# Weight products as plain float32 matmuls and one weight stream over all stages, in a six-layer transformer on one core

## What is computed

```
def ec_moe(x, w_router, w_gate, w_up, w_down):
    aff = softmax(einsum('bnd,de->bne', x, w_router))
    gates, idx = top_k(swapaxes(aff, 1, 2), cap)
    xin = x[bidx, idx]
    h = silu(einsum('becd,edf->becf', xin, w_gate)) * einsum('becd,edf->becf', xin, w_up)
    out = einsum('becf,efd->becd', h, w_down) * gates[..., None]
    return zeros_like(x).at[bidx, idx].add(out)

def swiglu(h, w_gate, w_up, w_down):            # four times, 1024 -> 2816 -> 1024
    return (silu(h @ w_gate) * (h @ w_up)) @ w_down

proj = h @ w_in        # in every mixer, 1024 -> 1536 to 6656 outputs
y = mixed @ w_out      # in every mixer, 1024 to 2304 -> 1024
```

## Time and profile before

| | |
|---|---|
| median of 3 runs | 2966.36 us (2957.82 to 2967.57) |
| profiled execution, its span | 2972.5 us (the profile gives no other time for it) |
| TensorE busy | 2382.3 us, 80% of the span |
| VectorE, ScalarE busy | 1300.9 us, 980.6 us |
| mean granted TensorE clock | 0.884 of full |
| moved by DMA | 690 MB |

### The profile page before, as it was taken

How to read it: one execution, slowest core, us unless ns; L and a number is a source line. 1 busy time by engine, 2 the same in 40 slices (tenths; PEclk the granted TensorE clock), 3 DMA queues, 4 the chain that set the end, 5 groups by cost and what they waited for, 6 DMA issues and landing times. The chain is left out here.

```text
span 2972.5 us, 33569 instructions
## 1 busy us (share of the span) xinstructions
PE 2382.3 (80%) x13393; PEld 1740.5 (59%) x13393; DVE 1300.9 (44%) x2056; ACT 980.6 (33%) x1638; POOL 22.4 (1%) x18
## 2 busy tenths in 40 slices
PE   8887555657876656649888988899879999987998
PEld 7752111126642213118767777787768888875887
DVE  5630000035622000024664554675667567465674
ACT  4420000015510000013444433544555454433543
POOL 0010000000010000000000000000000000000000
PEclk9977778778978778777988999999999999987999
DMA  6469999974469999984423443454236545561453
GB/s 229 158 270 421 421 422 422 421 297 159 192 278 419 420 420 419 422 312 116 117 83 132 144 159 127 132 198 156 90 121 210 193 142 198 159 195 33 159 198 121
DMA packets 277072, 689.98 MB, mean 232 GB/s; under 512 B 22193, under 2 KB 181889, under 8 KB 227664
## 3 DMA queue, kind: packets, MB, share of 16 engines
q1 hardware_dynamic: 276944, 688.20, 61.6%
HBM read 687.09 MB, written 5.28 MB: 233 GB/s over the span
## 5 line engine op out<-in xcount | busy, mean ns | idle before, releaser
L339 DVE TENSOR_TENSOR weight_quarters<-weight_ring,weight_quarters 128x1024 fp32r<-128x1024 f32 (+4 forms) x512 | 605.6, 1190 | 578.9 <-ACT weight_quarters L328 566.0
L328 ACT CAST weight_quarters<-weight_ring 128x1024 fp32r<-128x1024 f32 (+4 forms) x512 | 520.6, 1022 | 699.2 <-PE accumulators L3283 242.1
L3281 PE MATMUL accumulators<-xT_halves,weight_quarters 128*128 128x512 f32 x1408 | 497.7, 398 | 9.3 <-DVEq L3337 9.3
L1671 PE MATMUL accumulators<-weight_ring,arena 128*32 128x512 f32 x2048 | 333.6, 812 | 202.5 <-DMA weight_ring<-in_moe_w_up 101.7
L3283 PE MATMUL accumulators<-xT_halves,weight_quarters 128*128 128x256 f32 x1408 | 396.9, 282 | 0.0
L966 PE MATMUL accumulators<-weight_quarters,arena_halves 128*128 128x512 f32 x1552 | 362.2, 394 | 8.8 <-PEq L220 8.8
L1671 PEld LDWEIGHTS accumulators<-weight_ring,arena 128*32 128x32 f32 x2048 | 87.8, 143 | 436.9 <-issue 436.2
L966 PEld LDWEIGHTS accumulators<-weight_quarters,arena_halves 128*128 128x128 f32 x1552 | 295.4, 191 | 72.0 <-issue 9.9
L3281 PEld LDWEIGHTS accumulators<-xT_halves,weight_quarters 128*128 128x128 f32 x1408 | 266.2, 189 | 72.6 <-issue 10.0
L2423 PE MATMUL accumulators<-xT_halves,weight_quarters 128*128 128x256 f32 x2040 | 276.9, 298 | 15.1 <-DVE weight_quarters L339 10.9
L2423 PEld LDWEIGHTS accumulators<-xT_halves,weight_quarters 128*128 128x128 f32 x2040 | 267.2, 205 | 22.0 <-issue 9.9
(11 more groups left out here) (429 smaller groups left out, 2096.7 us busy)
## 6 DMA issues: line engine op xcount, KB each, us to landing
weight_ring<-in_moe_w_gate SPq DMA_DIRECT2D x64, 2048.0 KB, 19.7
weight_ring<-in_moe_w_up SPq DMA_DIRECT2D x64, 2048.0 KB, 21.1
weight_ring<-in_moe_w_down SPq DMA_DIRECT2D x64, 2048.0 KB, 21.4
weight_ring<-in_ffn_w_gate SPq DMA_DIRECT2D x44, 1024.0 KB, 5.3
weight_ring<-in_ffn_w_up SPq DMA_DIRECT2D x44, 1024.0 KB, 7.8
weight_ring<-in_ffn_w_down SPq DMA_DIRECT2D x20, 2048.0 KB, 7.9
weight_ring<-in_l_w_in SPq DMA_DIRECT2D x13, 2048.0 KB, 7.6
weight_ring<-in_mlstm_w_in SPq DMA_DIRECT2D x6, 2048.0 KB, 7.8
```

Source lines behind the costliest of these rows:

```text
L328: act.copy(high, raw).then_inc(self.m.high_ready, 1)
L339: dve.tensor_tensor(low, raw, high, ALU.subtract).then_inc(self.m.low_ready, 1)
L1671: last = pe.matmul(acc[e * CAP:(e + 1) * CAP, half * BANK:(half + 1) * BANK], tokens, w4[e][:, c * D + half * BANK:c * D + (half + 1) * BANK],
L3281: pe.matmul(out.rearrange("p (x t) -> p x t", x=2), gs.quarter(k, 0)[:, c, :], m.xT_r[:, :, c, :], start=(c == 0), stop=False)
```

## The change

- **Products.** Every weight product, every score of the mLSTM and every gather becomes one plain float32 matmul from the operands as they are. All casts and differences go, with the quarters, `Order`, the cross terms of the feed-forward layers, and the parts of activations. Activations are written once into `xT`, by ScalarE for some chunks and VectorE for the others (`moved`).
- **Stream.** The ring has 13 slots of 8 KiB per partition (1 MiB). All units of all stages stand in one list, `m.units`, and unit i goes to slot i mod 13. `fill` lets SP issue loads up to 13 units ahead of a point, each waiting until the unit 13 before it is used. A unit is one or two pieces of a column block (4 or 8 channel chunks), two chunks of rows, half of a feed-forward pair, or 256 rows of one expert. The loops are unrolled.
- **Feed-forward.** Weights are stationary (128x128), the 256 tokens move; gate and up of a unit take one bank each; ScalarE's silu reads PSUM, VectorE multiplies straight into `hT`.
- **Experts.** Group 0 is gathered first, the other three together in two calls of 384 columns (`gather_rest`), behind steps 4 and 8 of group 0.
- **Order of loads.** The orders of outputs that casts made in the even layer are now made by the transfer (pieces of 64 columns). The first stage loads five units, not two, ahead of the constants. The bias tiles of the selected stage are issued by POOL, not SP; the memory rows of the second expert layer at its start.
- **Pool layer.** Its projection writes the transposed form directly, so the transposing stage and the stage of parts go.

The core of the diff:

```diff
-SLOTS = 6
-SLOT = 4096
+SLOTS = 13
+SLOT = 2048
+    def load_units(self, sp, end):
+        while self.issued < min(end, len(self.units)):
+            stream, u = self.units[self.issued]
+            if self.issued >= SLOTS:
+                sp.wait_ge(self.unit_used, self.issued - SLOTS + 1)
+            stream.load(sp, u)
+            self.issued += 1
...
-PASSES = ((0, 0), (0, 1), (1, 0))
...
 def out_matmuls(m, stream, pe, s, chunks, lhs, bank, hidden=None, before=None):
-        for n, (xp, wp) in enumerate(PASSES):
-            ins = pe.matmul(m.ps[:, bank + 2 * t + h, :], lhs(xp, i, t), stream.quarter(i % 4, wp)[:, h * BANK:(h + 1) * BANK],
-                            start=(first and n == 0), stop=(last and n == 2))
+        return pe.matmul(m.ps[:, bank + 2 * t + h, :], lhs(i, t), stream.slot(i // 2)[:, i % 2 * D + h * BANK:i % 2 * D + (h + 1) * BANK], start=first, stop=last)
...
     def quarter(self, pe, s, u, k):
-        stream.wait_low(pe, g, j, k)
-                for n, (xp, wp) in enumerate(PASSES):
-                    last = pe.matmul(self.block(u, i), stream.quarter(k, wp, self.width(u))[:, c, i * P:(i + 1) * P], m.xT_r[:, xp, 2 * k + c, :], ...
+        for c in (2 * k, 2 * k + 1):
+            stream.begin_chunk(pe, u, c)
+            def turned(i):
+                return pe.matmul(self.block(u, i), stream.chunk(u, c)[:, i * P:(i + 1) * P], m.xT[:, c, :], ...
...
 def ffn(m, gu_stream, down_stream, tail):
-                    for c in range(DC):
-                        pe.matmul(out.rearrange("p (x t) -> p x t", x=2), gs.quarter(k, 0)[:, c, :], m.xT_r[:, :, c, :], ...
-                        last = pe.matmul(out[:, T:2 * T], gs.quarter(k, 1)[:, c, :], m.xT_r[:, 0, c, :], ...
+                    for f in range(2):
+                        for c in range(DC):
+                            last = pe.matmul(out[:, f * T:(f + 1) * T], w[:, c, f * P:(f + 1) * P], m.xT[:, c, :], ...
+                act.activation(gate[:, u % 2, :], m.ps[:, u % 2 * 2, :], ACT.Silu).then_inc(s["silu_out"], 1)
...
 def moe(m, stream, layer, tail, under=None):
+            def gather_rest(r):
+                for c in range(HALF):
+                    last = gather(HALF * r + c, m.ps[:, 4 + c, 0:REST], slice(P, P + REST))
+                last.then_inc(s["gathered"], 1)
...
 def selected_attention(m, in_stream, out_stream, tiles, tail):
-            heads.load(sp, s, 0)
-            heads.load(sp, s, 1)
-            in_stream.load_rest(sp)
+            in_stream.fill(sp, in_stream.n)
+        @block.gpsimd
+        def _(pool):
+            pool.wait_ge(m.bias_stored, 32)
+            for i in range(len(units)):
+                heads.load(pool, s, i)
```

More of the change, by code:

```diff
@@ L228 @@
 class Stream:
[L232 to L254, removed]
-        m.queue.append(self)
@@ L257, in slot @@
[L257 to L338, removed]
-        dve.tensor_tensor(low, raw, high, ALU.subtract).then_inc(self.m.low_ready, 1)
-        if k == 3 or last:
-            dve.wait_ge(self.m.low_ready, q + 1)
-            dve.sem_inc(self.m.unit_used, 1)
@@ L457, with __init__, place, slot @@
-PASSES = ((0, 0), (0, 1), (1, 0))
+    def __init__(self, m, units):
+        self.m, self.parts, self.n, self.base = m, units, len(units), len(m.units)
+        self.full = []
+        for u, parts in enumerate(units):
+            m.units.append((self, u))
+            m.loads[self.place(u)] += 16 * len(parts)
+            self.full.append(m.loads[self.place(u)])
+        m.queue.append(self)
+    def place(self, u):
+        return (self.base + u) % SLOTS
+    def slot(self, u):
+        return self.m.ring[:, self.place(u), :]
@@ L977, in out_matmuls @@
             for h in range(2):
-                last = products(i, t, h, i == 0, False)
-        last.then_inc(m.quarter_used, 1)
-    stream.wait_low(pe, 0, 0, chunks - 1)
+                last = product(i, t, h, i == 0, False)
+        if i % 2 == 1:
+            last.then_inc(m.unit_used, 1)
+    stream.wait_loaded(pe, chunks // 2 - 1)
     if hidden:
@@ L1052, in _ @@
         def _(act):
-            for i in range(stream.ready_made, chunks):
-                stream.high_part(act, i // 8, i // 4 % 2, i % 4)
-            stream.high_ahead(act)
             tail.warm_root(act, s)
@@ L3358, in after @@
-            def after(k, g, j):
-                if k == 1:
-                    gate_sum(g, j)
-                if k == 3:
-                    hidden(g, j)
-            def unit(g, j):
-                for k in range(first(g, j), 4):
-                    gs.low_part(dve, g, j, k)
-                    if not (isinstance(g, int) and g == 0 and j == 0):
-                        after(k, *back(g, j))
-            gs.each(dve, unit, peel=True)
-            for i in range(FFC):
-                ds.low_part(dve, i // 8, i // 4 % 2, i % 4, last=(i == FFC - 1))
-                if i < 4:
-                    after(i, *end)
```

1202 lines of the change are left out of this document (395 added, 807 removed).

## The result

The changed kernel takes 3169.9 us (median of 4 runs, 3169.5 to 3171.6); the kernel before took 2967.0 us on the same chip. The ratio is 1.068, 95% interval 1.066 to 1.071: slower by 203 us, forecast +213. The profiled execution's span is 3169.8 us.

A forecast was written before the change was run, and what follows sets the result against it. TensorE was taken to bound most stages outside the expert layers, weight transfer those layers. Products +331, start +4, removed work and waits -122 give +213 us on 2966, about 3180 us, range 3115 to 3235 (0.70).

The forecast's parts named there:

- Price of the product: Weight products outside the experts: plain 0.4275 us per 256 columns, split gate/up 0.345; TensorE +331 us in sum.
- Feed-forward: Four feed-forward layers: gate and up +29 us, down +16 us each, +180 us in all; removing casts and subtractions worth nothing.
- Mixers' idle time: TensorE's waits in mLSTM, GLA, even, odd and selected: 68 of 115 us go, bounds 0 and 115.
- Half-clock stretches: GLA, even and selected, at lowered clock after waits: fewer waits give back about 15 us, bounds 0 and 40.
- After the expert layers: Tails: 11 us saved after the second expert layer, 4 after the first; SP's loads ahead cost 0, at most 5 a stage.
- Experts: Expert layers: a larger ring shortens the transfer that sets the end, 2.5 us saved each; merged gathers 0.
- Narrow rows: Two units of the even layer loaded in rows of 256 bytes: 0 taken, between 0 and 10 us.
- Pool, tails: Pool layer: three units +7 us, transposes and parts stage -7.5; seven RMS tails 1.7 us less each.
- Signs: Profile marks named beforehand: two records a product, 0.214 us a record, feed-forward layer 228 us, ScalarE and VectorE near 430 and 620.
- Rivals 1 and 2: Waits outside the expert layers vanish almost wholly, 3050 us (chance 0.12); the mixers' waits stay, 3255 us (chance 0.09).
- rival 3: Expert layers: weight stream slower with 1 MiB transfers, 386 GB/s instead of 420, 85 us more, 3265 us; chance 0.05.
- rival 4: Products outside the experts: a plain product costs half of what was counted, about 2400 us in all; chance 0.03.

The follow-up runs named there:

- experiment 2: Kernel before, three matmuls a product kept, casts and subtractions of weights narrowed to 8 columns from the first gated layer on: 2903.5 us, ratio 0.978.
- `before_light`: Kernel before with weight casts and subtractions narrowed to 8 columns of each row from the first gated layer on, matmuls and waits kept: 2903.5 us, ratio 0.978.

## Why the prediction was right, and where its terms were off

It forecast +213 us and +203 were measured, and the likeliest case was the one that happened: TensorE sets the stages outside the experts, the plain product costs what the old rows say, and some of the waits go. That the sum came out only 10 us off is in part luck: the loads ahead of two stage ends cost 29 us more than forecast, and three other terms gave back 42 us more.

- **Price of the product.** 0.4275 us was read from a few old products; 0.432 is measured (a layer's 704 records of gate and up run from 1916.37 to 2068.39 us). The split gate/up product, read as 0.345 us from one dense stretch, took 0.347 to 0.358 over the four layers. TensorE's busy time outside the expert layers rose from 2382.3 - 613.3 = 1769.0 to 2643.3 - 586.8 = 2056.5 us, +287.5. The 331 of the sum less what the higher clock gave back (39.5, below) are 291.5.
- **Feed-forward.** +45 us less a shorter tail was forecast per layer; +39.7, 43.4, 42.2 and 40.1 came. For gate/up and for down the sum had +29 and +16 us; the starts of the first layer's products give +26 and +16. That the parts are worth nothing there is shown by experiment 2.
- **Mixers' idle time.** Forecast 68 of 115 us, measured 79.
- **Half-clock stretches.** Forecast 15 us in GLA, even and selected, bound 40. This term was too small. A lower clock costs nothing while TensorE stands idle, so what counts is its busy time x (1 - granted clock): in the stretches of these three it is 49.5 us before and 25.5 after, 24 given back, and in all five 64.5 and 32.3. Outside the expert layers as a whole it is 101.2 and 61.7, the 39.5 us above.
- **After the expert layers: the step that failed.** The forecast was -11 us behind the second one and -4 behind the first, from VectorE's part of the tail; measured were +9.9 and +4.0. VectorE's stand of 7.95 us did go, but I put SyncE's fill at 0 to 5 us, because little is in flight there. Twelve MiB ahead of a stage's end hold the end itself. With the fill capped the gaps are 18.9 and 8.5 us, 10.2 and 3.6 under the kernel before, so the two terms of the tail were right and the fill is what was mis-sized: it cost 20 and 8 us. That is 29 us off, against 11 us (mixers' idle time), 24 (clock) and 6.5 (experts) that gave more than forecast.
- **Start.** +4.3 us, forecast +4.
- **Experts.** -3.4 and -8.1 us, forecast -2.5 each; 420 GB/s with 1 MiB transfers, as forecast. The Trainium skill ("DMA: Bandwidth & Descriptors", section Bandwidth, Measured) gives 341 GB/s for 1 MB; with several in the queue, the trace shows 420.
- **Narrow rows.** Forecast 0 (0 to 10), measured 6.
- **Pool, tails.** The sum gave the pool stage 7 us of units, 5.8 of output products (8 of the 60 chunks), -7.5 and a tail of -1.7, +3.6 in all; +5.2 measured. From a feed-forward tail's first transpose to the next product it is 5.9 us where it was 7.6 to 8.0, 1.7 to 2.1 us less against 1.7 forecast.
- **Signs.** Two records a product, 0.216 us a record (0.214 forecast), 32 records of 512 columns in 13.9 us (13.7) and feed-forward stages of 233 us (228 and a tail) came as named; ScalarE and VectorE came out at 386 and 523 us, lower than the 430 and 620 named.

Rivals 1 and 2 lay on either side (3050 and 3255 us) and neither end of the waits was reached; rival 3 is refuted by the transfer rate, rival 4 by the record's 0.216 us.

The Trainium skill ("FP8 and Floating Point Precision", section TensorE Precision Notes) counts four passes for true float32. The measured series agrees, with its plain product 8% under four separate passes.

## What to carry to other kernels

A plain float32 product costs TensorE more (0.432 us for 256 columns of gate and up here, where the split one took about 0.35) and spares two other engines their work; it is worth it only in stages where TensorE waits for them. Read the idle time and the granted clock of each stage, not of the whole. Where a stage ends with all engines meeting, limit what the issuing engine still has to put into a full queue; the bytes ahead of the meeting point decide, and capping them took 28 us out of two gaps here, of 39 in all. None of the kernels run with the whole computation beat the kernel before; by the table, plain products in GLA, even and selected with capped fills, and split ones elsewhere, would be the version to try, which was not done.

## What the runs showed of the hardware beyond what I expected

- An issue of SyncE takes as long as the queue ahead: the same 41 loads in 34.3 and, begun 18.3 us sooner, 50.5 us.
- Weight loads of 192 ns follow each other every 0.112 us.
- Four float32r passes over 256 columns (a matmul of 512, two of 256) cost 0.465 us where a plain float32 product of 256 columns costs 0.430, both by records in a stretch of 100 us.
- With the same matmuls, TensorE's busy time outside the expert layers fell by 20 us when 50 us of its waits went (`before_light`), at a higher granted clock.
